# Re-timing the router steps of a one-core streaming encoder kernel, with more buffers for cached keys and late query weights

## The chip, the cores and the metric

The kernel runs on one core of a Trainium2 chip. Five engines take part, each with its own in-order queue: TensorE (PE), VectorE (DVE), ScalarE (ACT), GpSimd (POOL, which issues the gathers) and SyncE (SP, which issues all other transfers). They are held together by semaphores alone. The metric is the device time of one execution in microseconds.

## The reference

One inference step of a one-layer encoder for 384 tokens: 256 of a prompt and 128 of 8 running streams (16 tokens each, 512 cached). All is float32. The tokens lie in three tiles of 128 (tiles 0 and 1 the prompt, tile 2 the streams).

```python
h = rmsnorm(x, ln1_g)
q_a, k_a, v_a, q_i, k_i, w_i, q_b, k_b, v_b, g_b = project(h, w_in)
o_a = dsa(q_a, q_i, w_i, k_a, v_a, k_i)      # indexer scores, top-k keys, softmax attention
o_b = retention_mix(q_b, k_b, v_b, g_b, ...) # recurrent state, group norm, silu gate
x = x + concat([o_a, o_b]) @ w_out
h2 = rmsnorm(x, ln2_g)
# PEER: 8 heads, each chooses 16 of 128 * 128 experts for every token
s1, s2 = q[:, :, 0] @ keys1.T, q[:, :, 1] @ keys2.T
v1, i1 = top_k(s1, 16); v2, i2 = top_k(s2, 16)
top_s, sel = top_k(v1[:, None] + v2[None, :], 16); gate = softmax(top_s)
x = x + einsum('thk,thkd->td', gate * gelu(einsum('thkd,td->thk', exp_u[e], h2)), exp_v[e])
y = rmsnorm(x, ln_final_g)
```

## The kernel before

After a start that computes tile 0 up to the first two router results, the kernel is one long loop over 384 picks n, in all four compute queues. A unit u is one head of one tile (u = 8 t + h, 24 of them), and has 16 picks. For pick n:

- POOL (`gather`, L467 to L477) issues an indirect transfer of 128 rows of 2048 floats (u and v of two experts for each of 64 tokens; even picks serve the lower half of the tile, odd ones the upper) into one of G = 8 places; from the ninth on it waits until TensorE has summed the pick eight before (`acc`). At n = 16 u it waits for the unit's ids (`picked`).
- DVE makes the dot product with h2 (L1726), waiting for the row to land.
- ACT (`weigh`) makes gelu, the gate's weight, and a 128 by 64 diagonal of it.
- PE (`add_experts`) takes two picks at a time: four pairs of fp32 matmuls of the diagonals with the v rows, added up in PSUM banks 6 and 7; then it signals `acc`.

All other work is hung into this loop by hand. Each engine has a `Clock`; a generator does `yield from until(k)` and goes on after that engine's pick k. The numbers are the picks of each engine's own order, so an engine that is ahead of another by some picks reaches the same number earlier. PE ticks on even n only.

The router of unit u goes through the engines in this order: PE `query_part` (8 parts of 2 matmuls, from `q_at(u)`; two parts a tick, four where the unit is in HURRIED), ACT `take_q` (from PSUM bank 4), PE `query_scores` (at `scores_at(u)`, bank 5), DVE `top16` (15 steps, one a tick, two for some units; the first reads the scores, L1420; the fourth signals `topped`), ACT `gate_exp`, PE `spread_out` (a matmul that lays ids and gates out, bank 4), DVE `spread_take` (four small copies, L1489 and L1490, signals `picked`). Before, for most units: queries at 16 u - 40, taken at +7, scores at +10, top-16 at +11, spread at 16 u - 12, taken at 16 u - 10.

The weights of the queries come in loads of 2 MB, one for two to four units, all into `wt` slot 0: `load_q(k)` on SP waits until the last unit of the load before has its queries. SP is one queue, so each load also stands behind what is ahead of it there.

Beside this, `background` generators run attention and retention of tile 1 (picks 0 to 75), the indexer and retention of tile 2 (72 to 130), and the attention of tile 2 over the cached keys of the 8 streams (from ATT2 = 150, six picks a stream, keys and values in two buffers). At the end of a tile DVE waits for the tile's last sum, copies it into x (L1731) and ACT squares it for the final norm; PE starts the next tile's sum when that copy is made.

The change touches `ckv`, `w_q`, the timing functions, SP's `load_q` and `load_ckv`, `query_part`, `query_scores`, `spread_out`, the generators of the router on three engines, `attend_2` and its partners, and the tile ends.

Of the kernel before, what the change touches and what calls it, by code (L numbers as in the profile page):

```python
# [23 lines left out]
P = 128  # L24
# [59 lines left out]
def build(nc, a, o):  # L84
    with ExitStack() as ctx:
# [141 lines left out]
        ckv = (at(C, 2048, 1024), at(C, 3072, 1024))  # L227
# [28 lines left out]
        w_q = slot(wt[:, 0, :])  # L256
# [5 lines left out]
        w_in = {n: sem("w_" + n) for n in ("kv", "qi", "qa", "vb", "qkb", "gb", "out0", "out1", "out", "q")}  # L262
# [5 lines left out]
        ckv_in = [sem(f"ckv_in{i}") for i in range(2)]  # L268
# [41 lines left out]

        def q_at(u):
            return {2: 4, 3: 12, 16: 224}.get(u, 16 * u - 40)

        HURRIED = (2, 3, 16)

        def scores_at(u):
            return q_at(u) + (6 if u in HURRIED else 10)

        q_psum, sc_psum, spread_psum = ps[:, 4, 0:256], ps[:, 5, 0:256], ps[:, 4, 256:320]
# [20 lines left out]
        def _(sp):  # L340
# [19 lines left out]
            def load_q(k):  # L360
                if k > 0:
                    sp.wait_ge(q_ps, [u for u in range(UNITS) if q_load(u) < k][-1] + 1)
                sp.dma_start(wt[:, 0, :], a[f"w_q{Q_LOADS[k]}"]).then_inc(w_in["q"], 16)
# [53 lines left out]
            def load_ckv(b):  # L417
                for k in range(2):
                    sp.dma_start(ckv[b % 2][:, k * PAST:(k + 1) * PAST], a["ckv"][b][k]).then_inc(ckv_in[b % 2], 16)
# [4 lines left out]
            for b in range(2, STREAMS):  # L424
                sp.wait_ge(pv_ps, ATT[2] + b - 1)
                load_ckv(b)
                if b == 5:
                    load_q(6)
            sp.wait_ge(pv_ps, ATT[2] + STREAMS)
            sp.dma_start(x[:, 2, :], a["x"][2]).then_inc(x_again[2], 16)  # L430
            sp.wait_ge(hready, 2 * TILES)
            sp.dma_start(gfb, a["ln_final_g"].partition_broadcast(P)).then_inc(gf_in, 16)
            twice(2)
            sp.wait_ge(y_out, 1)
            sp.dma_start(o["y"][0], x[:, 0, :]).then_inc(y_done, 16)
            load_q(7)
            load_q(8)
            sp.wait_ge(y_out, 2)
            sp.dma_start(o["y"][1], x[:, 1, :]).then_inc(y_done, 16)
            load_q(9)  # L440
# [7 lines left out]
        def _(pool):  # L448
# [31 lines left out]
            for n in range(UNITS * KP):  # L480
# [13 lines left out]
                if n == 138:  # L494
# [3 lines left out]
                if n == 222:  # L498
                    take_rstd(H2_STAT[2])
                if n == 266:  # L500
# [4 lines left out]
        def _(pe):  # L505
# [203 lines left out]
            def query_part(u, part):  # L709
                t, h = divmod(u, HP)  # L710
                if part == 0:
# [7 lines left out]
                    if u >= 2:  # L719
                        pe.wait_ge(picked, max(2, u - 1))  # L720
                    pe.wait_ge(w_in["q"], 16 * (q_load(u) + 1))
                e, c0 = part // 4, part % 4 * 2
                col = (h % 2) * 256 + e * P
                for c in (c0, c0 + 1):
                    last = mm(q_psum[:, e * P:(e + 1) * P], w_q[:, c, col:col + P], h2T[:, c, :], c == 0, c == KC - 1)
# [7 lines left out]
            def query_scores(u):  # L733
                if u == 0:
                    pe.wait_ge(keys_in, 32)
                if u >= 1:
                    pe.wait_ge(topped, u)
                pe.wait_ge(q_sb, u + 1)
# [4 lines left out]
            def spread_out(u):  # L743
                pe.wait_ge(chosen, u + 1)
                pe.wait_ge(q_sb, 2 if u < 2 else min(u + 2, UNITS))
                mm(spread_psum, pair[:], spread.rearrange("p j e k -> p (j e k)")).then_inc(spread_ps, 1)
# [40 lines left out]
            def next_queries():  # L787
                for u in range(2, UNITS):
                    yield from until(q_at(u))
                    for part in range(8):  # L790
                        query_part(u, part)
                        if part % 4 == 3 or part % 2 and u not in HURRIED:
                            yield
                    yield from until(scores_at(u))
                    query_scores(u)

            def next_spreads():
                for u in range(2, UNITS):
                    yield from until(16 * u - 12)
# [156 lines left out]
            def scores_2(b):  # L956
# [8 lines left out]
                pe.wait_ge(ckv_in[b % 2], 32 * (b // 2 + 1))  # L965
                lhs = qzb[:, b, :, :, :]
                mm(ps[:, 0, :], lhs, ckv[b % 2][:, 0:PAST], True, False)
# [12 lines left out]
            def values_2(b):  # L980
                pe.wait_ge(pt_sb, PT[2] + b + 1)
                for c in range(5):
                    lhs = ckv[b % 2][:, PAST + c * P:PAST + (c + 1) * P] if c < 4 else kvnat[2][:, P:2 * P]
# [36 lines left out]
            def later_background():  # L1020
# [9 lines left out]
                for b in range(STREAMS):  # L1030
                    yield from until(ATT2 + 6 * b)
                    scores_2(b)
                    if b > 0:
                        prob_t2(b - 1)
                        yield
# [3 lines left out]
                yield  # L1039
# [6 lines left out]
            gens = (next_spreads(), next_queries(), background(), later_background(), index_2(), projections())  # L1046
# [7 lines left out]
        def _(act):  # L1054
# [122 lines left out]
            def next_queries():  # L1177
                for u in range(2, UNITS):
                    yield from until(q_at(u) + (5 if u in HURRIED else 7))
                    take_q(u)  # L1180

            def next_gates():
                for u in range(2, UNITS):
                    yield from until(16 * u - 20 if u > 2 else 15)
# [57 lines left out]
            def background():  # L1242
# [37 lines left out]
                for b in range(STREAMS):  # L1280
                    yield from until(ATT2 + 4 + 6 * b)
                    exp_2(b)
                    if b > 0:
                        yield
# [508 lines left out]
```

## Time and profile before

| | |
|---|---|
| median of 3 runs | 1324.73 us (1322.51 to 1324.82) |
| profiled execution | 1324.76 us, span 1323.0 us |
| mean granted TensorE clock | 0.832 |
| gathers | 384, from 147.9 to 1295.4 us |
| HBM read | 456.73 MB, 348 GB/s over the span |

The span is from the first to the last instruction of the profiled execution. "Busy" counts only the engine's own work, not its waits. The idle time before an instruction is put down to what released it. L507 is the helper through which all matmuls go, L1056 the one for all ScalarE operations, so these are told apart by their tiles.

### The profile page before, as it was taken

The page shows a single profiled execution, that of the slowest core. Times are in us where ns is not written, and L with a number is a line of the kernel's source. Part 1 is how long each engine was busy: PE and PEld are TensorE (multiplying, and loading weights), DVE is VectorE, ACT ScalarE, POOL GpSimd, SP SyncE. Part 2 cuts the span into 40 slices and gives each one's busy share as a digit, 9 for nine tenths or more (in the row PEclk, how much of TensorE's full clock was granted, in tenths as well). Part 3 has the DMA queues.
Part 4 walks back from the last instruction along what each step waited for, and adds up shares of the span by engine and source line. Part 5 has one row for each costly group of instructions (what it writes and reads, how often), then busy time and mean ns, then how long its engine had stood idle before and what let it go on. Part 6 is the DMA issues. An engine that isn't in the chain of part 4 may idle for free.

```text
span 1323.0 us, 12047 instructions
## 1 busy us (share of the span) xinstructions
PE 912.8 (69%) x3668; PEld 413.5 (31%) x3676; DVE 811.6 (61%) x2103; ACT 482.4 (36%) x1444; POOL 455.3 (34%) x405
## 2 busy tenths in 40 slices
PE   6999686886776866566577576865666566665654
PEld 4856543332233323222133232321222122221110
DVE  2242747865665768868557657557567665676543
ACT  2121243444334433323455445233244333433432
POOL 0000143343343433333333233242445344544440
PEclk9999898998888978677788887977888777877676
DMA  9511589999999999798999997999999999999995
GB/s 378 238 64 32 195 364 377 401 359 424 392 379 352 407 347 399 290 322 306 413 370 372 405 355 276 378 327 401 391 422 390 417 410 413 420 392 391 417 421 216
DMA packets 67793, 463.92 MB, mean 351 GB/s; under 512 B 8720, under 2 KB 10512, under 8 KB 15760
## 3 DMA queue, kind: packets, MB, share of 16 engines
q0 software_dynamic: 55296, 402.68, 76.6%
q1 hardware_dynamic: 12432, 60.47, 12.1%
q8 instruction: 29, 0.48, 0.1%
q14 instruction: 36, 0.29, 0.1%
HBM read 456.73 MB, written 3.24 MB: 348 GB/s over the span
## 4 chain that ended last, share of the span: by engine, by line
PE 39%; DVE 22%; DMA 16%; ACT 11%; issue 9%; POOL 2%; SPq 0%; POOLq 0%; DVEq 0%
PE ps L507 38%; DMA rows<-in_uv,ids 16%; DVE rows L1726 9%; ACT L1056 4%; ACT work L1056 3%; POOL rows L477 2%; ACT wgt L1056 2%; ACT zact L1056 1%; DVE work L1432 1%; DVE wt L1341 1%; DVE top L1337 1%; ACT wt L1056 1%; PE ps L510 1%; DVE work L1424 1%; DVE work L1436 1%
## 5 line engine op out<-in xcount | busy, mean ns | idle before, releaser
L507 PE MATMUL ps<-rows,work 128*64 128x512 f32 x1536 | 500.1, 787 | 370.4 <-ACT work L1056 369.9
L477 POOL DMA_INDIRECT rows<-in_uv,ids x384 | 437.8, 1140 | 721.5 <-PE ps L507 626.9
L1726 DVE CUSTOM_DVE_ANT_0 rows<-rows,masks 128x1024 f32<-128x1024 f32 x256 | 313.4, 1226 | 131.8 <-DMA rows<-in_uv,ids 126.5
L507 PEld LDWEIGHTS ps<-rows,work 128*64 128x64 f32 x1536 | 115.5, 168 | 636.0 <-ACT work L1056 458.3
L1056 ACT ACTIVATE zact<-zdot 128x1 f32<-128x1 f32 x384 | 76.9, 200 | 542.6 <-DVE zdot L1726 541.2
L1726 DVE CUSTOM_DVE_ANT_0 rows<-rows,wt 128x1024 f32<-128x1024 f32 x128 | 156.6, 1226 | 32.5 <-DMA rows<-in_uv,ids 29.1
L507 PE MATMUL ps<-wt 128*128 128x512 f32 (+5 forms) x468 | 138.4, 441 | 4.0 <-DVE wt L1508 1.9
L1056 ACT ACTIVATE work<-pair,wgt 128x64 f32<-128x64 f32 x384 | 133.5, 348 | 12.5
L507 PEld LDWEIGHTS ps<-work,wt 128*128 128x128 f32 (+1 forms) x776 | 103.3, 210 | 83.1 <-issue 81.8
L507 PE MATMUL ps<-work,wt 128*128 128x128 f32 (+1 forms) x776 | 120.1, 306 | 0.9 <-ACT work L1056 0.9
L1056 ACT ACTIVATE wgt<-zact,gates 128x1 f32<-128x1 f32 x384 | 113.1, 295 | 12.4
L1420 DVE MAX8 work<-ps 128x8 f32<-128x128 f32 x48 | 11.9, 290 | 139.2 <-PE ps L507 139.2
L507 PEld LDWEIGHTS ps<-wt 128*128 128x128 f32 (+1 forms) x476 | 73.3, 194 | 53.9 <-issue 46.5
L1056 ACT ACT_TABLE_LOAD x66 | 84.7, 1283 | 1.9 <-PEq L1776 0.7
L1056 ACT ACTIVATE wt<-ps 128x512 f32<-128x512 f32 (+5 forms) x59 | 32.3, 556 | 89.2 <-PE ps L507 54.3
L1056 ACT ACTIVATE work<-ps 128x256 f32<-128x256 f32 (+2 forms) x49 | 16.9, 351 | 125.5 <-PE ps L507 121.8
L1489 DVE CAST ids<-ps 64x16 uint32<-64x16 f32 x48 | 8.3, 172 | 62.9 <-PE ps L507 62.6
L507 PE MATMUL ps<-wt,rows 128*128 128x128 f32 (+1 forms) x320 | 46.8, 309 | 0.0
L507 PEld LDWEIGHTS ps<-wt,rows 128*128 128x128 f32 x320 | 43.9, 203 | 2.7 <-issue 1.0
L1726 DVE DVE_READ_ACCUMULATOR2_ANT zdot<- 128x1 f32 x384 | 31.4, 82 | 0.0
L452 POOL TENSOR_TENSOR rstd<-ms,half 128x1 f32<-128x1 f32 x9 | 8.7, 968 | 61.4 <-DVE ms L1322 54.3
L507 PE MATMUL ps<-wt,work 128*128 128x512 f32 x64 | 29.4, 597 | 0.0
(134 smaller groups left out, 605.5 us busy)
## 6 DMA issues: line engine op xcount, KB each, us to landing
wt<-in_w_q SPq DMA_DIRECT2D x10, 2048.0 KB, 12.1
rows<-in_uv,ids POOLq DMA_INDIRECT x384, 11.0
rows<-in_w_out SPq DMA_DIRECT2D x2, 2048.0 KB, 31.5
wt<-in_w_out SPq DMA_DIRECT2D x2, 2048.0 KB, 15.3
wt<-in_ckv SPq DMA_DIRECT2D x16, 256.0 KB, 8.8
x<-in_x SPq DMA_DIRECT2D x5, 512.0 KB, 9.0
rows<-in_w_qi SPq DMA_DIRECT2D x1, 2048.0 KB, 14.3
rows<-in_w_qa SPq DMA_DIRECT2D x1, 2048.0 KB, 15.3
```

The costliest lines, as they stand in the source:

```text
L452: pool.tensor_tensor(rstd[:, n:n + 1], ms[:, n:n + 1], half4[:, 0:1], ALU.pow).then_inc(rsd, 1)
L477: pool.indirect_dma_start(row[s], None, a["uv"], bass.IndirectOffsetOnAxis(ap=ids[:, own(n // KP).start + n % KP:own(n // KP).start + n % ...
L507: return nc.tensor.matmul(out, lhsT, rhs, start=start, stop=stop)
L510: return nc.tensor.transpose(out, in_, ident[0:k, 0:k])
L1056: return nc.scalar.activation(*args, **kw)
L1337: then(V.max(out=top8[:], in_=score))
L1341: then(V.match_replace(out=score, in_to_replace=top8[:], in_values=score, imm_value=TAKEN))
L1420: ins = V.max(out=top[:, e, 0:8], in_=s[e])
L1424: ins = V.match_replace(out=rest[e], in_to_replace=top[:, e, 0:8], in_values=s[e], imm_value=TAKEN)
L1432: ins = V.max_index(topi[:, e, 0:8], top[:, e, 0:8], s[e])
L1436: ins = V.max_index(topi[:, e, 8:16], top[:, e, 8:16], rest[e])
L1726: V.tensor_tensor_reduce(row[s][:, 0:D], row[s][:, 0:D], h2r[t % 2][:, n % 2, :], 1.0, 0.0, ALU.mult, ALU.add, zdot[:, s:s + 1]).then_inc( ...
```

## The change

The picks at which the router's steps stand are moved: queries earlier (16 u - 48), taken 11 picks later, scores at 16 u - 34, top-16 three picks behind them, spread at 16 u - 10 and taken three picks later, with exceptions at the start and at the tile changes. The spread of units from 2 on goes to bank 5. Cached keys and values have four buffers. The query weights of the last three loads go to slots 3, 4 and 5 with semaphores of their own. The copy of a tile's sum and its square come after the first picks of the next tile. The diff, with little context; left out are four calls on POOL that move by one or two picks, and `ckv[b % 2]` and its semaphore read as `b % 4` in `scores_2` and `values_2`.

```diff
@@ -224,7 +224,7 @@
         probT2 = at(B, 6016, 640)
-        ckv = (at(C, 2048, 1024), at(C, 3072, 1024))
+        ckv = [at(C, off, 1024) for off in (2048, 3072, 0, 1024)]
@@ -253,19 +253,23 @@
-        w_q = slot(wt[:, 0, :])
+        def w_q(k):
+            return slot(wt[:, 0 if k < 7 else k - 4, :])
         w_qi, w_qa = slot(at(rowf, 0, SLOT)), slot(at(rowf, SLOT, SLOT))
...
-        w_in = {n: sem("w_" + n) for n in ("kv", "qi", "qa", "vb", "qkb", "gb", "out0", "out1", "out", "q")}
+        w_in = {n: sem("w_" + n) for n in ("kv", "qi", "qa", "vb", "qkb", "gb", "out0", "out1", "out")}
+        q_in = [sem(f"q_in{i}") for i in range(4)]
         x_in = [sem(f"x_in{t}") for t in range(TILES)]
...
         cki_in = [sem(f"cki_in{i}") for i in range(4)]
-        ckv_in = [sem(f"ckv_in{i}") for i in range(2)]
+        ckv_in = [sem(f"ckv_in{i}") for i in range(4)]
         h2r_in = [sem(f"h2r_in{t}") for t in range(TILES)]
@@ -308,15 +312,30 @@
+        AHEAD, HURRIED, FAST = (2, 15, 16), (2, 8, 16), (2, 3, 16, 17, 18)
         def q_at(u):
-            return {2: 4, 3: 12, 16: 224}.get(u, 16 * u - 40)
-        HURRIED = (2, 3, 16)
+            return {2: 0, 3: 6, 8: 88, 16: 224, 17: 230}.get(u, 16 * u - 48)
+        def take_at(u):
+            return q_at(u) + (5 if u in HURRIED else 11)
         def scores_at(u):
-            return q_at(u) + (6 if u in HURRIED else 10)
-        q_psum, sc_psum, spread_psum = ps[:, 4, 0:256], ps[:, 5, 0:256], ps[:, 4, 256:320]
+            return {2: 6, 3: 22, 16: 232, 17: 248}.get(u, 16 * u - 34)
+        def top16_at(u):
+            return scores_at(u) + 3
+        def gate_at(u):
+            return top16_at(u) + (5 if u in FAST else 10)
+        def spread_at(u):
+            return {2: 18, 15: 228, 16: 244}.get(u, 16 * u - 10)
+        q_psum, sc_psum = ps[:, 4, 0:256], ps[:, 5, 0:256]
+        def spread_psum(u):
+            return ps[:, 4 if u < 2 else 5, 256:320]
@@ -358,9 +377,9 @@
             def load_q(k):
-                if k > 0:
+                if 0 < k < 7:
                     sp.wait_ge(q_ps, [u for u in range(UNITS) if q_load(u) < k][-1] + 1)
-                sp.dma_start(wt[:, 0, :], a[f"w_q{Q_LOADS[k]}"]).then_inc(w_in["q"], 16)
+                sp.dma_start(wt[:, 0 if k < 7 else k - 4, :], a[f"w_q{Q_LOADS[k]}"]).then_inc(q_in[max(0, k - 6)], 16)
@@ -416,28 +435,32 @@
                 for k in range(2):
-                    sp.dma_start(ckv[b % 2][:, k * PAST:(k + 1) * PAST], a["ckv"][b][k]).then_inc(ckv_in[b % 2], 16)
+                    sp.dma_start(ckv[b % 4][:, k * PAST:(k + 1) * PAST], a["ckv"][b][k]).then_inc(ckv_in[b % 4], 16)
...
             load_q(5)
-            for b in range(2, STREAMS):
-                sp.wait_ge(pv_ps, ATT[2] + b - 1)
+            sp.wait_ge(mt_ps, TILES)
+            load_ckv(2)
+            load_ckv(3)
+            for b in range(4, STREAMS):
+                sp.wait_ge(pv_ps, ATT[2] + b - 3)
                 load_ckv(b)
-                if b == 5:
+                if b == 4:
                     load_q(6)
...
             sp.dma_start(x[:, 2, :], a["x"][2]).then_inc(x_again[2], 16)
+            load_q(7)
             sp.wait_ge(hready, 2 * TILES)
...
             twice(2)
+            sp.wait_ge(wout, 2 * TILES)
+            load_q(8)
             sp.wait_ge(y_out, 1)
             sp.dma_start(o["y"][0], x[:, 0, :]).then_inc(y_done, 16)
-            load_q(7)
-            load_q(8)
+            load_q(9)
             sp.wait_ge(y_out, 2)
             sp.dma_start(o["y"][1], x[:, 1, :]).then_inc(y_done, 16)
-            load_q(9)
             sp.wait_ge(y_out, 3)
@@ -716,13 +739,14 @@
                         pe.wait_ge(q_sb, u)
-                    if u >= 2:
-                        pe.wait_ge(picked, max(2, u - 1))
-                    pe.wait_ge(w_in["q"], 16 * (q_load(u) + 1))
+                    if u == 2:
+                        pe.wait_ge(picked, 2)
+                    k = q_load(u)
+                    pe.wait_ge(q_in[max(0, k - 6)], 16 * (k + 1 if k < 7 else 1))
                 e, c0 = part // 4, part % 4 * 2
...
                 for c in (c0, c0 + 1):
-                    last = mm(q_psum[:, e * P:(e + 1) * P], w_q[:, c, col:col + P], h2T[:, c, :], c == 0, c == KC - 1)
+                    last = mm(q_psum[:, e * P:(e + 1) * P], w_q(q_load(u))[:, c, col:col + P], h2T[:, c, :], c == 0, c == KC - 1)
                 if part == 7:
@@ -735,6 +759,8 @@
                     pe.wait_ge(topped, u)
+                if u >= 3:
+                    pe.wait_ge(picked, u if u - 1 in AHEAD else u - 1)
                 pe.wait_ge(q_sb, u + 1)
@@ -742,8 +768,11 @@
                 pe.wait_ge(chosen, u + 1)
-                pe.wait_ge(q_sb, 2 if u < 2 else min(u + 2, UNITS))
-                mm(spread_psum, pair[:], spread.rearrange("p j e k -> p (j e k)")).then_inc(spread_ps, 1)
+                if u < 2:
+                    pe.wait_ge(q_sb, 2)
+                elif u not in AHEAD:
+                    pe.wait_ge(topped, min(u + 2, UNITS))
+                mm(spread_psum(u), pair[:], spread.rearrange("p j e k -> p (j e k)")).then_inc(spread_ps, 1)
@@ -791,12 +820,15 @@
                             yield
+            def next_scores():
+                for u in range(2, UNITS):
                     yield from until(scores_at(u))
...
                 for u in range(2, UNITS):
-                    yield from until(16 * u - 12)
+                    yield from until(spread_at(u))
                     spread_out(u)
@@ -1032,18 +1064,18 @@
                         prob_t2(b - 1)
-                        yield
+                        yield from until(ATT2 + 6 * b + 4)
                         values_2(b - 1)
...
                 prob_t2(STREAMS - 1)
-                yield
+                yield from until(ATT2 + 6 * STREAMS + 4)
                 values_2(STREAMS - 1)
...
-            gens = (next_spreads(), next_queries(), background(), later_background(), index_2(), projections())
+            gens = (next_spreads(), next_scores(), next_queries(), background(), later_background(), index_2(), projections())
             for n in range(0, UNITS * KP, 2):
@@ -1176,12 +1208,12 @@
                 for u in range(2, UNITS):
-                    yield from until(q_at(u) + (5 if u in HURRIED else 7))
+                    yield from until(take_at(u))
                     take_q(u)
...
                 for u in range(2, UNITS):
-                    yield from until(16 * u - 20 if u > 2 else 15)
+                    yield from until(gate_at(u))
                     gate_exp(u)
@@ -1278,29 +1310,33 @@
                 for b in range(STREAMS):
-                    yield from until(ATT2 + 4 + 6 * b)
+                    yield from until(ATT2 + 5 + 6 * b)
                     exp_2(b)
                     if b > 0:
-                        yield
+                        yield from until(ATT2 + 7 + 6 * b)
                         values_2(b - 1)
-                    yield from until(ATT2 + 9 + 6 * b)
+                    yield from until(ATT2 + 10 + 6 * b)
                     prob_t2(b)
-                yield from until(ATT2 + 11 + 6 * (STREAMS - 1))
+                yield from until(ATT2 + 13 + 6 * (STREAMS - 1))
                 values_2(STREAMS - 1)
-                yield from until(ATT2 + 64)
+                yield from until(ATT2 + 65)
                 act.wait_ge(x1_done, 6)
...
                 h2_take(2)
+            def y_square(t):
+                act.wait_ge(y_read, t + 1)
+                square(Y_STAT[t], x[:, t, :], h2r[t % 2][:, 0, :])
...
                 clock.tick(n, *gens)
-                if n % (HP * KP) == HP * KP - 1:
-                    act.wait_ge(y_read, t + 1)
-                    square(Y_STAT[t], x[:, t, :], h2r[t % 2][:, 0, :])
+                if n == t * HP * KP + 3 and t > 0:
+                    y_square(t - 1)
+            y_square(TILES - 1)
@@ -1485,7 +1521,7 @@
                     r = slice(64 * q, 64 * q + 64)
-                    src = spread_psum[r, :].rearrange("p (j e c q) -> p e q c j", j=2, e=2, q=2)
+                    src = spread_psum(u)[r, :].rearrange("p (j e c q) -> p e q c j", j=2, e=2, q=2)
                     V.tensor_copy(ids[r, own(u)].rearrange("p (c j) -> p c j", j=2), src[:, 0, q, :, :])
@@ -1564,15 +1600,14 @@
                 for u in range(2, UNITS):
-                    start = scores_at(u) + 1
-                    yield from until(start)
+                    yield from until(top16_at(u))
                     for i, _ in enumerate(top16(u)):
-                        if u not in (2, 16) or i % 2:
+                        if u not in FAST or i % 2:
                             yield
...
                 for u in range(2, UNITS):
-                    yield from until(16 * u - 10)
+                    yield from until(spread_at(u) + 3)
                     spread_take(u)
@@ -1685,17 +1720,17 @@
                 for b in range(STREAMS):
-                    yield from until(ATT2 + 3 + 6 * b)
+                    yield from until(ATT2 + 4 + 6 * b)
                     row_max(ATT[2] + b, [psf[:, 0:640].rearrange("p (j n) -> p j n", j=1)], 0, 1)
-                    yield from until(ATT2 + 6 + 6 * b)
+                    yield from until(ATT2 + 7 + 6 * b)
                     scale_probs(ATT[2] + b, prob2[:, b % 2:b % 2 + 1, :], 0, 1)
-                yield from until(ATT2 + 60)
+                yield from until(ATT2 + 61)
                 add_mix(2, 0)
-                yield from until(ATT2 + 63)
+                yield from until(ATT2 + 64)
                 add_mix(2, 1)
-                yield from until(ATT2 + 66)
+                yield from until(ATT2 + 67)
                 mean_square(H2_STAT[2])
-                yield from until(ATT2 + 69)
+                yield from until(ATT2 + 70)
                 normed(h2, H2_STAT[2], 2, g2b, hready)
@@ -1707,15 +1742,19 @@
             def finals():
-                yield from until(132)
+                yield from until(134)
                 mean_square(Y_STAT[0])
...
                 normed(x[:, 0, :], Y_STAT[0], 0, gfb, y_out)
-                yield from until(260)
+                yield from until(262)
                 mean_square(Y_STAT[1])
-                yield from until(270)
+                yield from until(272)
                 normed(x[:, 1, :], Y_STAT[1], 1, gfb, y_out)
+            def y_take(t):
+                dve.wait_ge(acc, (t + 1) * HP * KP // 2)
+                then(V.tensor_copy(x[:, t, :], psf[:, 6 * 512:8 * 512]), y_read)
@@ -1725,10 +1764,10 @@
                                        zdot[:, s:s + 1]).then_inc(dotted, 1)
+                if n == t * HP * KP + 1 and t > 0:
+                    y_take(t - 1)
                 clock.tick(n, *gens)
-                if n % (HP * KP) == HP * KP - 1:
-                    dve.wait_ge(acc, (n + 1) // 2)
-                    then(V.tensor_copy(x[:, t, :], psf[:, 6 * 512:8 * 512]), y_read)
+            y_take(TILES - 1)
             mean_square(Y_STAT[2])
...

```

## Rows read from the trace of the kernel before

**Rows 1.** The page: busy time, the gather's DMA queue, the dot product's group.
```profile
PE 912.8 (69%) x3668; PEld 413.5 (31%) x3676; DVE 811.6 (61%) x2103; ACT 482.4 (36%) x1444; POOL 455.3 (34%) x405
...
q0 software_dynamic: 55296, 402.68, 76.6%
...
L1726 DVE CUSTOM_DVE_ANT_0 rows<-rows,masks 128x1024 f32<-128x1024 f32 x256 | 313.4, 1226 | 131.8 <-DMA rows<-in_uv,ids 126.5
```

**Rows 2.** Windows: stretch, length, engines' busy us (instructions), granted clock, DMA share, GB/s.
```profile
148.00:197.00 49.00, 35.28 (x182) 20.36 (x180) 29.73 (x77) 19.04 (x63) 18.32 (x17) 0.90 0.82 329
197.00:495.00 298.00, 223.42 (x868) 93.02 (x864) 194.72 (x530) 114.50 (x343) 112.91 (x101) 0.87 0.99 382
495.00:612.00 117.00, 71.32 (x289) 32.25 (x289) 93.02 (x229) 35.16 (x111) 39.60 (x35) 0.77 0.87 327
612.00:763.00 151.00, 100.41 (x417) 45.01 (x422) 102.61 (x266) 73.42 (x200) 50.88 (x48) 0.81 0.97 385
763.00:815.00 52.00, 34.43 (x146) 15.19 (x147) 30.55 (x78) 25.39 (x66) 17.80 (x16) 0.80 0.78 297
815.00:958.00 143.00, 96.44 (x362) 38.63 (x361) 88.72 (x227) 50.74 (x162) 54.38 (x50) 0.82 0.96 375
958.00:1258.00 300.00, 188.63 (x679) 67.69 (x677) 198.12 (x507) 116.98 (x372) 138.46 (x113) 0.78 1.00 408
1258.00:1306.00 48.00, 25.47 (x74) 5.68 (x76) 22.69 (x38) 16.05 (x57) 16.80 (x16) 0.77 1.00 417
```

**Rows 3.** The same view: state load, first copy of normed tile, state store.
```profile
469.00:480.00 11.00, 5.68 (x20) 1.88 (x20) 6.87 (x17) 1.69 (x6) 5.50 (x5) 0.78 0.93 255
400.00:411.00 11.00, 9.06 (x41) 4.67 (x42) 4.17 (x11) 3.29 (x10) 3.66 (x4) 0.69 1.02 279
579.00:587.00 8.00, 5.57 (x16) 1.15 (x12) 3.81 (x7) 1.69 (x6) 2.90 (x2) 0.71 0.90 243
```

**Rows 4.** Waits, whole span: who for whom, us in total, times, longest.
```profile
DVE work L1420 <- PE ps L507: 139.2, 23, 10.8
ACT work L1056 <- PE ps L507: 121.8, 24, 9.5
...
DVE ids L1489 <- PE ps L507: 62.6, 22, 6.1
```

**Rows 5.** Timelines of PE and DVE, 788 to 804 us: start, length, instruction, idle before.
```profile
788.15 1.94 PE L507 MATMUL ps<-rows,work 128*64 128x512 f32 x8
790.01 0.71 PE L507 MATMUL ps<-keysT,work 128*128 128x128 f32 x4
...
798.99 3.68 PE L507 MATMUL ps<-rows,work 128*64 128x512 f32 x8 [7.15 <-ACT work L1056]
...
790.76 0.50 DVE L1420 MAX8 work<-ps 128x8 f32<-128x128 f32 x2 [10.79 <-PE ps L507]
...
803.14 0.17 DVE L1489 CAST ids<-ps 64x16 uint32<-64x16 f32 x1 [6.09 <-PE ps L507]
```

**Rows 6.** Tiles: issue to landing, gathers first, then query weights.
```profile
DMA to landing us min/median/max: 5.4/11.0/27.5
...
DMA to landing us min/median/max: 7.6/12.1/17.0
```

**Rows 7.** Waits from 958 to 1258 us.
```profile
ACT work L1056 <- PE ps L507: 27.9, 6, 5.7
DVE work L1420 <- PE ps L507: 22.8, 6, 4.8
DVE ids L1489 <- PE ps L507: 21.8, 7, 3.7
```

**Rows 8.** Waits from 495 to 612 us.
```profile
DVE work L1420 <- PE ps L507: 10.5, 2, 5.3
...
DVE ids L1489 <- PE ps L507: 6.1, 2, 3.3
DVE x L1731 <- PE ps L507: 4.6, 1, 4.6
```

More of the change, by code:

```diff
@@ L493, in _ @@
                     group_rstd(2)
-                if n == 138:
+                if n == 140:
                     take_rstd(Y_STAT[0])
@@ L497, in _ @@
                     pool.memset(qzb, 0.0).then_inc(qzb_zero, 1)
-                if n == 222:
+                if n == 223:
                     take_rstd(H2_STAT[2])
-                if n == 266:
+                if n == 268:
                     take_rstd(Y_STAT[1])
@@ L964, in scores_2 @@
                     pe.wait_ge(expd, ATT[2] + b)
-                pe.wait_ge(ckv_in[b % 2], 32 * (b // 2 + 1))
+                pe.wait_ge(ckv_in[b % 4], 32 * (b // 4 + 1))
                 lhs = qzb[:, b, :, :, :]
-                mm(ps[:, 0, :], lhs, ckv[b % 2][:, 0:PAST], True, False)
+                mm(ps[:, 0, :], lhs, ckv[b % 4][:, 0:PAST], True, False)
                 mm(ps[:, 0, :], selb[:, b, :, :], bias2[:, 0:512], False, True)
@@ L982, in values_2 @@
                 for c in range(5):
-                    lhs = ckv[b % 2][:, PAST + c * P:PAST + (c + 1) * P] if c < 4 else kvnat[2][:, P:2 * P]
+                    lhs = ckv[b % 4][:, PAST + c * P:PAST + (c + 1) * P] if c < 4 else kvnat[2][:, P:2 * P]
                     last = mm(ps[:, 3, P:2 * P], lhs, probT2[:, c * P:(c + 1) * P], c == 0, c == 4)
```

## The prediction

> **What bounds the kernel now.** I read the page first: three engines are far from full (TensorE 69%, VectorE 61%, ScalarE 36% of the span), while one DMA queue, the gather of expert rows, holds the 16 DMA engines for 76.6% of it [rows 1]. Each pick fetches 128 rows of 8 KB, 1.05 MB, and there are 384.
>
> Second, the windows by stretch, cut at the picks' own limits: 148 us is the first gather, then gathers 16 to 111, 112 to 143, 144 to 191, 192 to 207, 208 to 255, 256 to 367, and the last 16 [rows 2]. The last stretch has nearly no background work and moves 417 GB/s at a DMA share of 1.00. I take that as the full rate. The time that a stretch loses against it is its length times (1 - GB/s / 417): 10.3, 25.0, 25.3, 11.6, 15.0, 14.4, 6.5 and 0 us, together 108 us. So the loop is bound by the gathers, with 108 us in which too little was in flight, and the 148 us ahead of it and 17 us after it are chains of their own.
>
> Not all of the 108 can come back. Short transfers lower the rate though the DMA engines are busy: the two copies of the normed tile (the one at 400 us, 279 GB/s, stands for both), the load of the retention state (255) and its store (243) [rows 3]. By the same rule these four windows lose 3.6 (counted twice, at some 3 for the second), 4.3 and 3.3 us, 14 in all. The ramp of 10.3 us starts from eight gathers that wait for the first experts' sum, and stays. That leaves 108 - 10 - 14 = 84 us that a better order could reach at most.
>
> Third, the waits [rows 4]. VectorE waits for TensorE 139.2 us at the scores (L1420, 23 times, 6.1 us each) and 62.6 us at the spread (L1489, 22 times, 2.8 us); ScalarE waits 121.8 us for work from TensorE, nearly all of it the queries (24 times, 5.1 us). All sit in the in-order queue that also carries the dot product or the diagonal of each pick. The code says why they are there: VectorE asks at pick s+1 for scores that TensorE issues after pick s, and TensorE can only finish pick s when VectorE and ScalarE are past s+1.
>
> Fourth, one such stall in order of time [rows 5]: TensorE ends pair and scores at 790.7, VectorE had waited 10.79 us for them, so TensorE's next pair is starved for 7.15 us, then runs in 3.68 us instead of the 1.94 us of the pair before it; VectorE waits 6.09 us again for the spread behind that pair. A gather waits for the sum of the pick eight before it, and takes 11.0 us in the median and 5.4 at least to land [rows 6], so a stall that outlasts what is in flight empties the DMA engines. The stretch with this stall ran at 297 GB/s.
>
> **The change, part by part.** *Scores.* VectorE's first step moves from one pick behind TensorE to three (3 instead of 1 after scores_at). Two more picks give TensorE at least two dot products' time [rows 1], 2 x 1.23 = 2.5 us, and at the full gather rate 2 x 1.05 MB / 417 GB/s = 5.0 us. Of 6.1 us that removes between 2.5 and 5.0, so 57 to 115 of the 139 us. *Spread.* From two picks behind to three: 1.2 to 2.5 us of 2.8, 27 to 55 of the 63 us. *Queries.* The last part is issued at q_at+6; ScalarE took it at +7, now at +11: four more picks, at least 4.9 us of 5.1. Nearly all of the 122 us goes. The first and hurried ones keep three picks.
>
> What is a removed wait worth? Two bounds. In the stretch from 958 us the three waits make 22.8 + 21.8 + 27.9 = 72.5 us and the loss is only 6.5: 0.09 us for each, since rows in flight cover them [rows 2, 7]. That ratio on the 206 to 292 us removed gives 19 to 26 us. From the other side, where VectorE is the bound, a wait costs its whole length: from 495 to 612 VectorE is busy 93.0 of 117 us and waits 10.5 + 6.1 + 4.6 = 21.2 for TensorE, so busy and waiting fill the stretch [rows 2, 8]. There the gain is nearly one to one.
>
> *Spread in the scores' bank.* The matmul and four copies keep their sizes. TensorE no longer waits for a query two units on, but for that unit's scores to be consumed (VectorE, two picks earlier in its own order); VectorE runs ahead of TensorE, so I cost it at 0, and at up to 2 us a unit if that cover goes. Query u loses its wait for picked; scores get it instead, five picks after the spread was taken: 0.
>
> *Tile change.* VectorE takes the finished sum after the first two dot products of the next tile, not before them. Two dots (2.5 us) move beside the wait of 4.6 us at the first tile end [rows 8] and the like one at the second; the third tile end is unchanged. 2 to 5 us for both, counted in the stretches. ScalarE's square goes four picks later and waits for nothing.
>
> *Cached keys.* Four buffers for the eight streams: the same 16 DMAs of 256 KB. No wait of TensorE for them stands in the rows of before, so no gain; the loads of streams 2 and 3 move ahead of the attention. SP is in order: load_q(6) now sits behind stream 4 and ahead of stream 5, and waits for query 13 (TensorE pick 166); stream 5 is needed at 180. Hidden by 14 picks.
>
> *Late queries' slots.* The loads for units 18 to 23 go to free slots and no longer wait for earlier queries: three of 2 MB, the same bytes. They took 12.1 us in the median, 17.0 at most [rows 6], against 10 picks of cover (25 us) before; nothing was late, so 0. But unit 4 gets short cover: its load waits for query 3, now done at pick 12, and query 4 starts at 16. Two pairs are 10 to 13 us against 12.1: a wait of 0 to 5 us, once. I take 2.
>
> *Attention steps* shift one or two picks. values_2 at +4 instead of +2 lets ScalarE's copy be there when TensorE asks: up to 1 us a stream, 0 to 8, in the stretches below.
>
> **The sum, by stretch** (what can be reached after the short transfers, and what I take). 197 to 495: 25.0 - 7.9 = 17, VectorE not the bound and DMA share 0.99: 7, less 2 for unit 4, so 5. 495 to 612: 25.3 - 3.3 = 22; waits of 21.2 in the bounding engine: 14. 612 to 763: 11.6, take 5. 763 to 815: 15.0 for the one stall chain shown, take 9. 815 to 958: 14.4 - 3.0 = 11, take 4. 958 to 1258: 6.5, take 2. Together 39 us. The profiled execution took 1324.76 us, span 1323.0, and the median of the runs is 1324.73, so nothing is to be corrected: 1324.8 - 39 = **1286 us**.
>
> A pair behind a stall takes 3.68 us and one in flow 1.94, and the granted clock is 0.80 in that stretch [rows 2, 5]: the two levels, 1.2 and 2.4 GHz. The Trainium skill says the same ("TensorE: Matmul & The Clock Gate", What's actually happening): throttled is the default, activity releases it. By that rule spreading the work evenly could keep the engine at the lower level rather than free it. Even then a pair of 3.68 us is under the 5.0 us that the gathers of a pair need, so the rule makes a round longer by 1.7 us but leaves the sum where the DMA bounds it. The clock of 0.78 in the nearly full stretch from 958 us agrees [rows 2].
>
> **Rivals.** *A: the rows in flight hid most of it.* The stalls only shift, and the ratio of the last stretch, 0.09, holds nearly everywhere outside VectorE's own bound. For it: the DMA share is 0.96 to 0.99 in three stretches of tiles 0 and 1. Against it: 0.87 and 0.78 in the two worst. Gain 5 to 20 us, middle 14: 1311 us.
>
> *B: slower, late ids.* The spread now leaves TensorE at 16u-10 and is taken at 16u-7; the gather 16u may go when pair 16u-8 is summed, so one pair (1.94 to 3.68 us) is the cover for a small matmul and four copies of 0.17 [rows 5]. If background work on VectorE (score rounds, state updates) comes between, the gather waits for the ids and the DMA engines run dry once per unit. It decides from 39 / 22 = 1.8 us late per unit; at 2.3 us it costs 51: 1324.8 - 39 + 51 = 1337 us. Against it: the spread is first among VectorE's steps of a pick, and the dot of 16u-7, ahead of it, is needed for pair 16u-8 anyway.
>
> *C: it does not do what it says.* VectorE catches up three picks in no time because their rows have long landed (dots at 1.23 us each), and waits at the new place as long as at the old: the 10.8 us waits would stay 8 us, and the chain only moves. 1325 us, within the noise.
>
> **Chances.** Forecast (25 to 55 us less) 0.62; A 0.24; C 0.06; B 0.08. Its own range is 1270 to 1300; to hold 8 of 10 it reaches into A and toward the 84 us bound, half of it: 1262 to 1314. Faster by over 0.2% (2.6 us, about what a measurement of this kernel can tell from none): 0.62 + 0.24 = 0.86; within 0.06; slower 0.08.
>
> **What would show it.** Right: waits at L1420 for TensorE under 60 us, at the spread under 30, ScalarE's for queries near 10; the stretch of gathers 112 to 143 near 103 us instead of 117 and 192 to 207 near 43 instead of 52; the last 128 gathers nearly as long as before. TensorE waiting for w_q near pick 16 for a few us. Wrong: waits of POOL for the copies of the spread (B), or the three waits gone and the gathers still far under 417 GB/s, with VectorE's or TensorE's own work filling the time (A).

## The result, and the profile after

The changed kernel took 1256.6 us in the median of 4 runs (1254.1 to 1257.6), the kernel before 1323.6 (1319.6 to 1324.8): ratio 0.9496, 95% interval 0.9469 to 0.9522. That is 67 us less. The forecast was 1286 us, 39 less, with a range from 1262: the direction held, the size did not, and the time lies under the range.

The windows of the changed kernel, cut at the same picks as [rows 2], with the same columns:

```profile
148.00:197.00 49.00, 36.58 (x193) 22.50 (x192) 33.88 (x100) 19.04 (x63) 16.68 (x17) 0.90 0.82 324
197.00:483.00 286.00, 224.40 (x878) 94.80 (x877) 190.25 (x512) 115.08 (x340) 115.05 (x100) 0.90 1.00 392
483.00:583.00 100.00, 64.90 (x292) 29.62 (x292) 94.09 (x230) 35.67 (x112) 37.57 (x35) 0.83 0.97 393
583.00:717.00 134.00, 95.74 (x412) 42.93 (x413) 97.54 (x251) 70.98 (x191) 50.31 (x48) 0.80 1.01 419
717.00:759.00 42.00, 31.33 (x156) 15.30 (x154) 34.45 (x91) 28.12 (x74) 17.58 (x17) 0.92 1.01 421
759.00:907.00 148.00, 96.36 (x356) 37.34 (x356) 85.79 (x204) 52.95 (x167) 55.73 (x50) 0.82 1.01 404
907.00:1190.00 283.00, 184.56 (x650) 62.20 (x650) 201.33 (x527) 117.14 (x371) 121.28 (x114) 0.78 1.01 417
1190.00:1239.00 49.00, 28.41 (x76) 6.24 (x78) 24.33 (x39) 16.06 (x57) 16.35 (x16) 0.67 0.94 387
```

By the same rule, length times (1 - GB/s / 417), the stretches now lose 10.9, 17.1, 5.8, -0.6, -0.4, 4.6, 0 and 3.5 us, 41 in all where they lost 108. The difference is 67 us: the whole gain. (The 3.5 of the last stretch is its end: the first 25 us of it run at 421 GB/s, and the last 6, which reach past the last landings, at 167.) The engines' own work is the same (VectorE 94.1 us in the third stretch, 93.0 before); the stretches are shorter, not emptier. The sixth is 5 us longer and the seventh 17 shorter in part because two query loads of 2 MB, 10 us at the full rate, moved out of the seventh into the sixth.

The waits over the whole span, to be held against [rows 4] and against these two of the kernel before:

```profile
PE ps L507 <- ACT work L1056: 371.4, 130, 9.2
DVE rows L1726 <- DMA rows<-in_uv,ids: 155.6, 127, 4.8
```

After:

```profile
PE ps L530 <- ACT work L1088: 310.6, 141, 8.7
DVE rows L1765 <- DMA rows<-in_uv,ids: 293.0, 260, 5.9
...
DVE work L1456 <- PE ps L530: 19.4, 12, 7.9
ACT work L1088 <- PE ps L530: 14.4, 7, 4.6
DVE ids L1525 <- PE ps L530: 14.3, 6, 5.2
...
PE ps L530 <- DMA wt<-in_w_q: 4.4, 1, 4.4
```

L1456 is the scores' wait (139.2 us before, now 19.4), L1525 the spread's (62.6, now 14.3), and ScalarE's is that for the queries (121.8, now 14.4). TensorE's own wait for ScalarE's diagonals fell from 371.4 to 310.6 us, 61 us less. What VectorE now waits for is the landing of rows: 293.0 us, 260 times (155.6 before), which is what an engine does that is ahead of a busy DMA. The last row is unit 4's short cover: its load was issued at 209.7 us and TensorE could go on at 221.4.

The place of the stall of [rows 5], where unit 13's spread is made and taken, in the timelines of TensorE and VectorE:

```profile
746.28 1.94 PE L530 MATMUL ps<-rows,work 128*64 128x512 f32 x8 [1.89 <-ACT work L1088]
...
751.50 1.94 PE L530 MATMUL ps<-rows,work 128*64 128x512 f32 x8 [1.07 <-ACT work L1088]
753.37 0.43 PE L530 MATMUL ps<-work,pair 128*128 128x64 f32 x2
...
753.62 1.22 DVE L1765 CUSTOM_DVE_ANT_0 rows<-rows,wt 128x1024 f32<-128x1024 f32 x1
754.77 0.16 DVE L1525 CAST ids<-ps 64x16 uint32<-64x16 f32 x1
```

The spread ends on TensorE at 753.8; VectorE reaches the copies at 754.77, right behind a dot, and waits for nothing. The pairs take 1.94 us each and TensorE's gaps are 1 to 2 us, not 7.

### The profile page after: what moved, and what is told of

Read it like the earlier page. It is cut to its first block, busy times and chain, and to the rows that moved or that the text cites. A ratio compares the mean times of both kernels' runs of the same rounds, so it can differ in the third digit from the quotient of the medians.

```text
span 1255.6 us, 12036 instructions
## 1 busy us (share of the span) xinstructions
PE 900.1 (72%) x3676; PEld 407.6 (32%) x3676; DVE 812.7 (65%) x2103; ACT 486.1 (39%) x1444; POOL 436.7 (35%) x405
## 4 chain that ended last, share of the span: by engine, by line
DMA 44%; PE 28%; DVE 15%; issue 5%; ACT 4%; POOL 3%; SPq 0%; DVEq 0%; POOLq 0%
DMA rows<-in_uv,ids 43%; PE ps L530 27%; DVE rows L1765 7%; POOL rows L500 3%; ACT work L1088 1%; ACT wgt L1088 1%; DMA wt<-in_w_q 1%; PE ps L533 1%; DVE wt L1377 1%; DVE top L1373 1%; ACT zact L1088 1%; ACT L1088 1%; ACT wt L1088 0%; DMA half<-in_half 0%; DVE work L1486 0%
## 5 line engine op out<-in xcount | busy, mean ns | idle before, releaser
L530 PE MATMUL ps<-rows,work 128*64 128x512 f32 x1536 | 488.1, 768 | 309.5 <-ACT work L1088 309.1
L500 POOL DMA_INDIRECT rows<-in_uv,ids x384 | 418.6, 1090 | 679.2 <-PE ps L530 585.8
L530 PEld LDWEIGHTS ps<-rows,work 128*64 128x64 f32 x1536 | 111.2, 162 | 581.0 <-ACT work L1088 413.1
L530 PE MATMUL ps<-wt 128*128 128x512 f32 (+4 forms) x476 | 141.5, 442 | 2.9 <-DVE wt L1544 1.9
L530 PEld LDWEIGHTS ps<-work,wt 128*128 128x128 f32 (+1 forms) x776 | 100.0, 204 | 69.1 <-issue 67.9
L530 PE MATMUL ps<-work,wt 128*128 128x128 f32 (+1 forms) x776 | 114.9, 297 | 5.3 <-DMA wt<-in_w_q 4.4
L479 POOL TENSOR_TENSOR rstd<-veps,half 128x4 f32<-128x4 f32 x3 | 4.4, 1456 | 70.1 <-DVE veps L1427 70.0
L1456 DVE MAX8 work<-ps 128x8 f32<-128x128 f32 x48 | 11.9, 290 | 19.7 <-PE ps L530 19.4
L530 PE MATMUL ps<-x,wt 64*128 64x128 f32 (+4 forms) x100 | 22.7, 346 | 2.0 <-DVE x L1552 2.0
```

The costliest lines, as they stand in the source:

```text
L479: pool.tensor_tensor(rstd4[:], veps[:], half4[:], ALU.pow).then_inc(o_rstd, 1)
L500: pool.indirect_dma_start(row[s], None, a["uv"], bass.IndirectOffsetOnAxis(ap=ids[:, own(n // KP).start + n % KP:own(n // KP).start + n % ...
L530: return nc.tensor.matmul(out, lhsT, rhs, start=start, stop=stop)
L1456: ins = V.max(out=top[:, e, 0:8], in_=s[e])
```

## The experiments

Ratios are to the kernel before on the same chip, with their 95% intervals; us are the ratio's difference times 1320. The edits are to the changed kernel, but for four runs where the text says that they are to the kernel before. The theory at the start was the forecast's, that three waits carried most of the lost time; the rival, that buffers, tile ends and the attention's order did.

**All distances old.**

```diff
 def take_at(u):
-    return q_at(u) + (5 if u in HURRIED else 11)
+    return q_at(u) + (3 if u in HURRIED else 7)
 def top16_at(u):
-    return scores_at(u) + 3
+    return scores_at(u) + (3 if u in (17, 18) else 1)
-        yield from until(spread_at(u) + 3)
+        yield from until(spread_at(u) + 2)
```

> The changed kernel with the old distances behind TensorE alone: queries taken 1 pick after their last part, top-16 one pick after the scores (units 17 and 18 keep three), spread taken two picks after it. Where the steps stand on TensorE, the bank, the buffers and the tile ends stay changed. Theory 1 (the three waits were most of the lost time): the waits at the scores, the queries and the spread come back to some 250 us and the time to about 1300 us, 45 us over the changed kernel, ratio 0.983. Theory 2 (buffers, tile ends and the attention's order brought most): the waits come back but the time stays under 1275 us, ratio under 0.963.

Measured 1281.5 us, ratio 0.9728 (0.9661 to 0.9794): 31 us lost by ratio, 25 by medians, between the two theories. Waits at the scores 109.1, at the queries 87.3 and at the spread 50.6 us.

**One distance each** (the first, second and third edit above, alone):

> Only the top-16's distance is put back to one pick (units 17 and 18 keep three). Theory 1: waits of VectorE at the scores near 100 us again, and 15 to 25 us of the 67 lost: 1272 to 1282 us. Theory 2: rows in flight cover a single wait per unit: under 5 us, at most 1262 us.

> Only ScalarE's taking of the queries is put back, from 5 picks behind their last part to 1 (hurried units from 3 to 1). Theory 1: ScalarE waits near 100 us again for queries and the time rises by 10 to 20 us: 1267 to 1277 us. Theory 2: under 5 us, at most 1262 us.

> Only the taking of the spread is put back from three picks behind it to two. Theory 1: VectorE's wait there rises from 14 to about 40 us, the time by 3 to 8 us: 1260 to 1265 us. Theory 2, and also the fear that late ids cost something: no loss, or a gain of up to 3 us, since the ids come earlier: 1254 to 1258 us.

Top-16: 1275.7 us, 0.968 (0.9618 to 0.9743), 24 us lost (19 by medians). Queries: 1257.7 us, 0.9531 (0.947 to 0.9593), nothing that can be told from none. Spread: 1259.8 us, 0.955 (0.9488 to 0.9611), likewise unclear. These intervals are wide, some 8 us either way, since the kernel before scattered from 1311 to 1328 us beside these runs. ScalarE's waits with the queries' distance old, and VectorE's with the top-16's old, from the two runs' waits:

```profile
ACT work L1088 <- PE ps L530: 102.1, 23, 7.7
```

```profile
DVE work L1456 <- PE ps L530: 97.2, 20, 9.1
```

Two waits of 100 us in the same loop. Held against each other, run beside run on one chip, VectorE's costs 18 us more than ScalarE's; against the changed kernel VectorE's costs 19 to 24 us, ScalarE's 1 to 5, which is not clear of none.

Both waits sit in front of work that TensorE needs next, so that alone does not explain the two prices. What the starved engine must still do before TensorE can go on does. The same place in both traces, first with the queries' distance old (ScalarE and TensorE), then with the top-16's (VectorE and TensorE):

```profile
1021.70 1.94 PE L530 MATMUL ps<-rows,work 128*64 128x512 f32 x8 [0.45 <-ACT work L1088]
1024.99 0.38 ACT L1088 ACTIVATE work<-ps 128x256 f32<-128x256 f32 x1 [3.34 <-PE ps L530]
1027.02 2.58 PE L530 MATMUL ps<-rows,work 128*64 128x512 f32 x8 [2.07 <-ACT work L1088]
```

```profile
1017.74 3.68 PE L530 MATMUL ps<-rows,work 128*64 128x512 f32 x8 [1.69 <-ACT work L1088]
1022.61 0.50 DVE L1456 MAX8 work<-ps 128x8 f32<-128x128 f32 x2 [5.87 <-PE ps L530]
1027.18 3.57 PE L530 MATMUL ps<-rows,work 128*64 128x512 f32 x8 [4.61 <-ACT work L1088]
```

When ScalarE's wait ends, at 1024.99, the next pair starts 2.0 us later: VectorE was making its dots meanwhile, and hardly more than the two diagonals is missing. From pair to pair that is 5.3 us, about the 5.0 us that two gathers take at the full rate. When VectorE's wait ends, at 1022.61, the next pair starts 4.6 us later, behind two dots of 1.23 us and then the diagonals: 9.4 us from pair to pair. Over nearly all of these waits (21 of the 23, 19 of the 20) the medians from the wait's end to the next pair are 2.3 and 5.6 us. So the first stall hides behind the gathers and the second does not. TensorE's whole wait for diagonals says the same: 311.6 us with the queries' distance old, 331.2 with the top-16's, 310.6 in the changed kernel.

**Tile ends, buffers, slots, attention order, one at a time.** The tile ends:

```diff
-                if n == t * HP * KP + 1 and t > 0:
-                    y_take(t - 1)
                 clock.tick(n, *gens)
+                if n % (HP * KP) == HP * KP - 1:
+                    y_take(t)
```

(and ScalarE's square likewise.) The buffers: `ckv` has two, with `b % 2` throughout, and on SP

```diff
-            sp.wait_ge(mt_ps, TILES)
-            load_ckv(2)
-            load_ckv(3)
-            for b in range(4, STREAMS):
-                sp.wait_ge(pv_ps, ATT[2] + b - 3)
+            for b in range(2, STREAMS):
+                sp.wait_ge(pv_ps, ATT[2] + b - 1)
                 load_ckv(b)
-                if b == 4:
+                if b == 3:
                     load_q(6)
```

The query slots: `w_q` and `load_q` use slot 0 for all ten loads, and loads 7 to 9 stand where they stood in the kernel before. The attention order: the numbers of `attend_2` and its partners as before, for example

```diff
-                        yield from until(ATT2 + 6 * b + 4)
+                        yield
                         values_2(b - 1)
```

> Only the tile ends are put back: VectorE copies the tile's sum before the next tile's dots, and ScalarE squares it at once. Theory 3 (the distances gave 25 of the 67 us, the rest is spread over the other parts): 2 to 6 us lost, 1259 to 1263 us, and a wait of 3 to 5 us at each copy again. Theory 4 (the rest is where the steps stand on TensorE and what they wait for there): within 3 us of the changed kernel for this and for the three kernels beside it.

> Only the cached keys and values go back to two buffers, with SP's loads in the old order (the query load of units 14 to 17 behind stream 3, since behind stream 5 it would come after its use). Theory 3: the loads come late for the new order of the attention, where values_2 is two picks later: TensorE waits for them, 5 to 15 us, 1262 to 1271 us. Theory 4: the loads of 9 us fit before their use: at most 1260 us.

> Only the last three query loads go back to slot 0 and behind the earlier queries, and to their old places on SP. Theory 3: with queries starting 8 picks earlier each load has less cover, and the one behind the first tile's output comes after its use: TensorE waits 5 to 15 us in all, 1262 to 1271 us. Theory 4: 0 to 3 us, at most 1260 us.

> Only the order of the stream attention on the three engines is put back (row max, exponentials and scaling one pick earlier, values two picks earlier on TensorE). Theory 3: TensorE waits for the copy of the transposed probabilities, up to 1 us a stream, and the engines wait for each other's step: 5 to 12 us, 1261 to 1268 us, all between picks 150 and 205. Theory 4: at most 1260 us.

Tile ends 0.9496 (0.946 to 0.9532): nothing. Slots 0.9454 (0.9424 to 0.9485) and attention order 0.9467 (0.9428 to 0.9506): nothing, or a loss of up to 0.4% that these parts of the change bring. Two buffers: 1278.0 us, 0.9634 (0.96 to 0.9669), 18 us lost. Its waits name the cause, and the timeline of TensorE shows three of the six:

```profile
DVE rowmax L1383 <- PE ps L527: 48.5, 7, 10.5
PE ps L527 <- DMA wt<-in_ckv: 45.6, 6, 9.7
```

```profile
680.88 2.04 PE L527 MATMUL ps<-wt 128*128 128x512 f32 x2 [9.71 <-DMA wt<-in_ckv]
701.56 2.47 PE L527 MATMUL ps<-wt 128*128 128x512 f32 x3 [6.49 <-DMA wt<-in_ckv]
725.20 2.05 PE L527 MATMUL ps<-wt 128*128 128x512 f32 x2 [8.69 <-DMA wt<-in_ckv]
```

**Two buffers with the old attention order, and the router's part alone** (the four groups of edits together):

> The changed kernel with two buffers for cached keys and the old attention order, all else changed. Theory 5: 1250 to 1260 us, TensorE's wait for cached keys (45.6 us with the new attention order) under 10 us. Theory 6: 1270 to 1280 us, a wait over 30 us.

> Everything but the router's part is put back at once: tile ends, cached keys in two buffers with SP's old order (query load of units 14 to 17 behind stream 3), query slots, attention order. Theory 5 (the router's re-timing made nearly the whole gain; four buffers are only needed because values_2 is two picks later): 1250 to 1262 us, and no wait of TensorE for cached keys. Theory 6 (the buffers bring 18 us in themselves): 1270 to 1280 us.

> As the kernel with the router's part alone, and the distances behind TensorE are old too (queries 1 pick, top-16 one, spread two). What is left of the change is where queries, scores and spread stand on TensorE, the spread's bank and the waits that go with it. Theory 5: 1275 to 1290 us: the positions carry 35 to 50 of the 67 us, the distances 25. If the positions carry nothing by themselves: 1315 us or more.

Two buffers and the old order: 0.9522 (0.9499 to 0.9546). The router's part alone: 0.9545 (0.9507 to 0.9584). So beside the router's part all the rest together brings some 0.5%, with overlapping intervals, and the four buffers pay mainly for the later values_2: TensorE waits 9.3 us for cached keys in two buffers with the old order, 45.6 with the new. With the old order, two buffers (0.9522) and four (0.9467) lie 7 us apart, their intervals just overlapping, so a small worth of their own is not excluded. The positions alone took 1304.5 us, between the two expectations: 0.9876 (0.9822 to 0.993), 16 us of gain, 44 short of the router's part. Taken out here, with nothing else to lean on, the distances cost 44 us and not 31. The same numbers read the other way: with the distances old, the rest (tile ends, buffers, slots, attention order) is worth 0.9876 - 0.9728, some 20 us (from runs on two chips), and with them new some 6 or nothing. The parts of the change stand in for each other, so no split of the 67 us among them is the only one.

**The distances put into the kernel before**, nothing else changed:

```diff
-                    start = scores_at(u) + 1
+                    start = scores_at(u) + 3
...
-                    yield from until(16 * u - 10)
+                    yield from until(16 * u - 9)
                     spread_take(u)
```

> The kernel before with two distances changed and nothing else: top-16 three picks behind the scores instead of one, spread taken three picks behind instead of two. If a distance is worth the same in both kernels (19 us for top-16, 3 for the spread, measured by taking it away): 1298 to 1306 us. If it is worth more there, where queries, scores and spread stand closer together: under 1290 us. If it only moves the wait: over 1315 us.

> The kernel before with the top-16 three picks behind the scores instead of one; nothing else. Theory 7 (a wait of VectorE costs by its length, since it holds the dots that TensorE, and so the scores themselves, need): the scores' wait falls from 139 to about 30 us, 110 us less at the 0.35 us per us that both distances together gave: 38 us, 1280 to 1290 us. Rival 8 (the two waits feed each other, so one alone brings little): over 1300 us.

> The kernel before with the spread taken three picks behind its matmul instead of two; nothing else. Theory 7: the wait there falls from 63 to about 15 us, 48 us less at 0.35: 17 us, 1300 to 1310 us. Rival 8: under 5 us, over 1315 us.

> The kernel before with the top-16 two picks behind the scores: half the step. Theory 7: TensorE works in pairs, and after the scores it needs the second dot of the next pair; at two picks that dot stands ahead of the wait, so TensorE can go on and most of the 38 us comes already: 1285 to 1300 us, though 60 to 90 us of the wait stay. If the gain is by the wait's length alone: half of it, about 1303 us.

Both: 1263.5 us, 0.9554 (0.9521 to 0.9588), 59 us. Top-16 alone: 0.9597 (0.9562 to 0.9632), 53 us. Spread alone: 0.9772 (0.9734 to 0.981), 30 us. Top-16 at two picks: 0.9747 (0.97 to 0.9795), 33 us. From the waits of these four, in this order:

```profile
ACT work L1056 <- PE ps L507: 112.2, 24, 9.6
DVE work L1420 <- PE ps L507: 27.7, 9, 7.9
DVE ids L1489 <- PE ps L507: 10.3, 6, 6.2
```

```profile
DVE ids L1489 <- PE ps L507: 36.0, 21, 6.5
DVE work L1420 <- PE ps L507: 33.8, 12, 7.9
```

```profile
DVE work L1420 <- PE ps L507: 137.6, 23, 11.6
...
DVE ids L1489 <- PE ps L507: 21.8, 12, 5.2
```

```profile
DVE work L1420 <- PE ps L507: 75.7, 20, 8.3
DVE ids L1489 <- PE ps L507: 43.7, 21, 5.4
```

The sum of VectorE's two waits falls from 201.8 us to 38.0, 69.8, 159.4 and 119.4: by 164, 132, 42 and 82, for 59, 53, 30 and 33 us of time, so 0.36, 0.40, 0.71 and 0.40 us for each us. Rival 8 falls: one alone does bring much. But theory 7's sizes missed too: it expected 38 us from the top-16's distance and 17 from the spread's by one price of 0.35, and 53 and 30 were measured. Each alone brings more than its share of the 59 together, and the waits show part of why: the top-16's distance also cuts the spread's wait from 62.6 to 36.0. What is left to lose is also less with every part. Whether a wait counts by its length or by the pick in which it falls the two-pick run does not tell, since length (139, 76, 34 us) and gain (0, 33, 53 us) go together. With both distances the kernel's loop runs at 399 GB/s in the profiled execution (1269.5 us, the slowest of the four):

```profile
148.00:1242.00 1094.00, 767.18 (x3005) 321.62 (x3013) 754.67 (x1943) 449.24 (x1361) 443.27 (x393) 0.83 0.99 399
```

1094 x (1 - 399 / 417) = 47 us lost, against 108 before and 41 in the changed kernel. ScalarE's 112.2 us for the queries are still there, and all that the rest of the change adds to these two numbers, ScalarE's distance among it, is 0.9554 - 0.9496, 8 us.

**A try at a faster version**, the old slots and the old attention order with four buffers:

> The changed kernel with the old query slots and the old attention order together, four buffers kept: a try at a version that is faster than both. Each alone measured 0.3 to 0.4% under the changed kernel, within its uncertainty. If both are real: 1248 to 1252 us, ratio near 0.943. If they were noise: 1256 us, 0.9496.

1254.0 us, 0.9502 (0.947 to 0.9534): the same as the changed kernel. What the two runs alone showed is within the noise, and no faster version was found.

## Why the prediction was wrong in size

- **The bound** (gathers; 108 us lost, 84 within reach): right. The gain of 67 is inside it, and it is found whole in the windows. The stretches named as signs came too: 100 us for gathers 112 to 143 (near 103 forecast) and 42 for 192 to 207 (near 43).
- **How much of the waits goes**: the scores' fell by 120 us (57 to 115 forecast), the spread's by 48 (27 to 55), the queries' by 107 (nearly all). Right, a little low at the scores.
- **What a removed wait is worth: the step that failed.** I had 0.09 us for each us from the stretch from 958 us, and 1 where VectorE is the bound, and lumped all three waits. The 39 us forecast for 206 to 292 us of removed waits are 0.13 to 0.19 for each. The runs show two prices. VectorE's waits at the scores and the spread cost 0.36 to 0.71 us for each us in the kernel before; ScalarE's for the queries cost 0.05 or nothing in the changed kernel (88 us more of it, 1 to 5 us of time, not clear of none), and in the kernel before it was not tested alone. Of VectorE's waits 168 us went, for 67 us of time: 0.40. The 0.09 was made from 72.5 us of waits, of which 27.9 were ScalarE's, in a stretch that had only 6.5 us to lose at all.
- **The sum by stretch**, where that price went in: from 197 us on the loss against the full rate fell by 8, 19.5, 12, 15, 10 and 6.5 us, where 5, 14, 5, 9, 4 and 2 stood. Every term was too low. From 495 us on nearly all came that I had called within reach (22, 12, 15, 11 and 6.5); only the stretch from 197 to 495 gave back no more than half of its 17. (The lengths changed by 12, 18, 17, 11, -6 and 17 us between the same gathers, but these hold transfers that moved.) The largest miss is 612 to 763, of which I took 5 without a reason, and from 197 on I had pointed at a DMA share of 0.99 [rows 2]. That share did not show the loss: 612 to 763 ran at 385 GB/s at 0.97 and runs at 419 at 1.01, and 382 GB/s stood beside 0.99.
- **Tile ends** 2 to 5 us: measured nothing. **Unit 4's load** 0 to 5 us of wait: 4.4, right. **Slots** 0: right. **Attention order** a gain of 0 to 8: nothing.
- **Cached keys** at 0: near right with the old attention order. I did not see that the later values_2 in the same change takes the cover from two buffers, which costs 18 us if they are not doubled: the same edit's other half.
- **The clock**: 0.78 in the seventh stretch before and after, and 0.842 over the run (0.832 before). It rose in the third and fifth stretches (0.77 to 0.83, 0.80 to 0.92), but the fourth and sixth lost 12 and 10 us less at an unchanged one (0.81 and 0.80, 0.82 and 0.82). So it was not what brought the gain there; no run tests it by itself.
- **Rival B, late ids**: did not come. GpSimd's only wait for the copies is the 29.6 us one at the start, as before, and taking the ids one pick earlier made nothing faster. **Rival A** (14 us) had the same error in full: its ratio of 0.09. **C** is refuted by the waits.

## What to carry to other kernels

Price a wait by how long its producer then stands still: here two dots and two diagonals lie between the end of VectorE's wait and TensorE's next pair (4.6 us), and only the diagonals behind ScalarE's (2.0 us), against 5.0 us that the gathers of a pair take. So one changed number (top-16 three picks behind the scores, not one) brings 53 us by itself, where the whole change brings 67, while as long a wait on ScalarE cost little or nothing. Read lost DMA time from GB/s against the best stretch of the same trace, not from the busy share. When a step moves later, look at which buffer it keeps full: the doubling that seemed idle was the price of the move.

## What the runs showed of the hardware that was not expected

Gathers of 1.05 MB ran beside 2 MB loads and the attention's 256 KB loads at 419 to 421 GB/s over 176 us (583 to 759), no less than with hardly anything beside them (417 in the last stretch of the kernel before). Their median time to land rose from 11.0 to 13.0 us while the loop got faster: by an estimate from the gathers' count, their time and these medians, some 4.6 were in flight on the mean instead of 3.7, so the longer time to land is not a slower memory.
